# Scores in pairs of tiles, a split mean square, half rows of x from two queues, and later small products in a two-layer encoder

## The reference

```python
for i in range(DEPTH):                       # DEPTH = 2
    h = (_chunked_spatial_gating if i % 2 == 0 else _diff_attention)(x, ...)
    x = _layer_norm(DEEPNORM_ALPHA * x + h, ln_g[i, 0], ln_b[i, 0])
    h = _conv_glu_ffn(x, ...)
    x = _layer_norm(DEEPNORM_ALPHA * x + h, ln_g[i, 1], ln_b[i, 1])
# the attention, per head h (8 heads) with two halves j of 64 channels:
logits = einsum('bqhjd,bkhjd->bhjqk', q, k) + bias
probs = softmax(logits);  attn = probs[:, :, 0] - lam * probs[:, :, 1]
o = einsum('bhqk,bkhe->bqhe', attn, v)
o = o * rsqrt(mean(square(o), axis=-1) + LN_EPS) * subln_g * (1 - lambda_init)
```

## Time and profile before

| | us |
|---|---|
| median of 3 runs | 1295.48 (1295.4 to 1296.23) |
| profiled execution | 1295.56 |
| its span | 1293.9 |
| PE busy | 1277.3 |
| DVE busy | 637.0 |
| ACT busy | 456.7 |
| POOL busy | 158.6 |

### The profile page before, as it was taken

The page is one execution under the profiler, slowest core; times in us unless marked ns, Lnnn a source line. Parts: engine busy times, 40 slices in busy tenths (PEclk is TensorE's granted clock), DMA queues, the critical chain, the costliest instruction groups (busy, mean ns, idle before and its releaser), DMA issues.

```text
span 1293.9 us, 15596 instructions
## 1 busy us (share of the span) xinstructions
PE 1277.3 (99%) x6078; PEld 1051.6 (81%) x6078; DVE 637.0 (49%) x879; ACT 456.7 (35%) x545; POOL 158.6 (12%) x159
## 2 busy tenths in 40 slices
PE   8999999999999999999999999999999999999997
PEld 6788888889888888888888777788888888888886
DVE  3627877346343434433463566664743434343346
ACT  3422333322232323322314677776132323232230
POOL 3001100040000000000315442434200000000001
PEclk9999999999999999999999999999999999999999
DMA  8334563250322332222513334234132223323221
GB/s 300 105 98 115 176 174 139 93 184 1 130 97 97 97 97 97 98 97 94 166 58 92 105 88 114 82 115 152 44 98 97 97 97 96 99 93 102 94 101 65
DMA packets 103931, 140.62 MB, mean 109 GB/s; under 512 B 9360, under 2 KB 81128, under 8 KB 103632
## 3 DMA queue, kind: packets, MB, share of 16 engines
q1 hardware_dynamic: 94304, 127.67, 30.5%
q0 software_dynamic: 9440, 12.11, 2.9%
q10 hardware_dynamic: 144, 0.26, 0.1%
HBM read 137.85 MB, written 10.52 MB: 115 GB/s over the span
## 4 chain that ended last, share of the span: by engine, by line
PE 94%; DVE 4%; issue 1%; ACT 1%; DMA 0%; SPq 0%; DVEq 0%; ACTq 0%
PE bank L1208 31%; PE bank L1212 30%; PE bank L1211 30%; PE bank L1570 1%; PE bank L1224 1%; PE bank L1430 1%; DVE xt_lo L731 1%; PE bank L1594 1%; DVE x_tok L785 1%; DVE r_stat L754 0%; ACT xt_hi L436 0%; DMA w_raw<-in_a_w_in_dram 0%; DVE x_tok L748 0%; DVE x_tok L776 0%; PE bank L1433 0%
## 5 line engine op out<-in xcount | busy, mean ns | idle before, releaser
L1208 PE MATMUL bank<-xt_hi,w_hi 128*128 128x512 f32 (+1 forms) x1008 | 383.3, 380 | 0.4 <-DVE xt_lo L731 0.4
L1212 PE MATMUL bank<-xt_hi,w_lo 128*128 128x512 f32 (+1 forms) x1008 | 378.9, 376 | 0.0
L1211 PE MATMUL bank<-xt_lo,w_hi 128*128 128x512 f32 (+1 forms) x1008 | 378.8, 376 | 0.0
L726 DVE TENSOR_TENSOR w_lo<-w_raw,w_hi 128x2048 fp32r<-128x2048 f32 x79 | 180.8, 2288 | 190.5 <-ACT w_hi L431 164.1
L1208 PEld LDWEIGHTS bank<-xt_hi,w_hi 128*128 128x128 f32 x1008 | 189.7, 188 | 36.6 <-issue 3.0
L1211 PEld LDWEIGHTS bank<-xt_lo,w_hi 128*128 128x128 f32 x1008 | 189.8, 188 | 35.3 <-issue 1.4
L1212 PEld LDWEIGHTS bank<-xt_hi,w_lo 128*128 128x128 f32 x1008 | 189.7, 188 | 34.5
L431 ACT CAST w_hi<-w_raw 128x2048 fp32r<-128x2048 f32 x53 | 101.2, 1912 | 191.2 <-PE bank L1208 188.6
L1208 PE MATMUL bank<-w_hi,s_hi 128*128 128x512 f32 x416 | 162.5, 391 | 0.0
L1212 PE MATMUL bank<-w_hi,s_lo 128*128 128x512 f32 x416 | 161.9, 389 | 0.0
L1211 PE MATMUL bank<-w_lo,s_hi 128*128 128x512 f32 x416 | 161.9, 389 | 0.0
(11 more groups left out here) (191 smaller groups left out, 1411.9 us busy)
## 6 DMA issues: line engine op xcount, KB each, us to landing
w_raw<-in_f_w_in_dram SPq DMA_DIRECT2D x44, 1024.0 KB, 5.1
w_raw<-in_f_w_down_dram SPq DMA_DIRECT2D x22, 1024.0 KB, 4.8
w_raw<-in_a_w_in_dram SPq DMA_DIRECT2D x14, 1024.0 KB, 5.9
bias_by_query_key<-bias_by_distance POOLq DMA_DIRECT2D x8, 1024.0 KB, 15.5
w_raw<-in_a_w_out_dram SPq DMA_DIRECT2D x8, 1024.0 KB, 4.9
w_raw<-in_b_w_qkv_dram SPq DMA_DIRECT2D x16, 512.0 KB, 5.1
bias_sb<-bias_by_query_key SPq DMA_DIRECT2D x32, 256.0 KB, 2.6
w_raw<-in_b_w_qkv_dram SPq DMA_DIRECT2D x4, 1024.0 KB, 5.2
```

The source lines that it names most:

```text
L726: dve.tensor_tensor(lo_of(u), w_raw[:, u % 2, :], hi_of(u), ALU.subtract).then_inc(w_lo_done, 1)
L1208: ins = pe.matmul(o, a_hi, b_hi, start=start, stop=False)
L1211: pe.matmul(o, a_hi, b_lo, start=False, stop=False)
L1212: return pe.matmul(o, a_lo, b_hi, start=False, stop=stop)
```

## The change

- `scores` of two tiles stand next to each other in PE's list, in four banks (2 and 3 for even tiles, 1 and 4 for odd ones); each waits for the tile two before it. Query and key are projected into banks 0 and 2. DVE's and ACT's lists are reordered to match; on ACT `query_key(1, 0)` now stands ahead of `exps(0, 3)`.
- The squares are written twice by ACT, fp32 and as a high part in float32r; DVE makes the low part (`square_lo`), and the mean square is two float32r products with float32r `ones`, in bank 0 (in bank 4 for the last two heads). They lie in the buffers of `at_hi` and `at_lo`, so `probs_hi` waits for `ms_mm`.
- The value pairs of heads 4 and 5 use banks 5 and 6, those of heads 6 and 7 both bank 0.
- x comes in half rows (2 KB), the first halves of tiles 0 and 1 from ACT's queue, the others from SP's between the weight pieces. PE, ACT and DVE take halves: PE's first part works through growing squares of tiles and channel blocks (`highs`, `lows`).
- The bias table's product is split in high and low (two float32r products for one fp32 product), and `small_products` stands in the middle of token group 2, in banks 4 to 6.
- POOL's low half of a unit is sliced between the `shares` of a head.

```diff
+        def query_key_bank(c):
+            return bank[2 * c]
+        def score_bank(t, j):
+            return bank[(1, 4)[j] if t % 2 else 2 + j]
+        def pair_bank(n):
+            return bank[5 + n - TB if n < TB + 2 else 0]
+        def square_bank(h):
+            return bank[0 if h < H - 2 else 4]
+        def squares_of(h):
+            return (sq_hi, sq_lo) if h < H - 2 else (sz_hi, sz_lo)
...
-            sp.dma_start(x_tok[:, 0, :], xv[0]).then_inc(x_landed[0], 16)
-            for c in range(4):
-                sp.dma_start(raw(0, NB)[:, c:c + 1, :], cols(a_w_in[0], WIDTH, NB, c, 1)).then_inc(w_piece[c], 16)
-            sp.dma_start(x_tok[:, 1, :], xv[1]).then_inc(x_landed[1], 16)
-            for c in range(2):
+            def x_half(t, h):
+                sp.dma_start(x_tok[:, t, NB * h:NB * h + NB], xv[t, :, NB * h:NB * h + NB]
+                             ).then_inc(x_landed[TB * h + t], 16)
+            def second_unit(c):
                 sp.dma_start(raw(1, NB)[:, 2 * c:2 * c + 2, :], cols(a_w_in[0], WIDTH, NB, 4 + 2 * c, 2)
                              ).then_inc(w_piece[4 + c], 16)
-            for t in range(2, TB):
-                sp.dma_start(x_tok[:, t, :], xv[t]).then_inc(x_landed[t], 16)
+            for c in range(4):
+                if c >= 2:
+                    x_half(c, 0)
+                sp.dma_start(raw(0, NB)[:, c:c + 1, :], cols(a_w_in[0], WIDTH, NB, c, 1)).then_inc(w_piece[c], 16)
+            x_half(0, 1)
+            second_unit(0)
+            second_unit(1)
+            for t in range(1, TB):
+                x_half(t, 1)
             load_tokens_side(a_w_in[0], WIDTH, U_AV, N_AV, 2)
...
+            def x_half(t, h):
+                act_e.wait_ge(turned, TB * h + t + 1)
+                act_e.copy(xt_hi[:, 4 * h:4 * h + 4, t * P:t * P + P],
+                           bank[4 + t][:, :].rearrange("p (k n) -> p k n", n=P)).then_inc(xt_hi_done, 1)
+            for t in range(2):
+                act_e.dma_start(x_tok[:, t, 0:NB], x[0].rearrange("(t p) d -> t p d", p=P)[t, :, 0:NB]
+                                ).then_inc(x_landed[t], 16)
+            for t in range(TB):
+                piece(t)
+                x_half(t, 0)
+            x_half(0, 1)
             piece(4)
             piece(5)
-            for t in range(2, TB):
-                split_rows(0, t)
+            for t in range(1, TB):
+                x_half(t, 1)
...
-                act_e.activation(o_sq[:, :], bank[7][:, :], ACT.Square).then_inc(sq_done, 1)
+                act_e.activation(o_sq[:, :], bank[7][:, :], ACT.Square)
+                if h >= H - 2:
+                    act_e.wait_ge(mixp_done, TB * (H - 1) + 1)
+                act_e.activation(squares_of(h)[0][:, :], bank[7][:, :], ACT.Square).then_inc(sq_hi_done, 1)
...
             weights(U_QK1)
+            values_hi(TB)
             exps(0, 0)
-            values_hi(TB)
             exps(0, 1)
+            values_hi(TB + 1)
             exps(0, 2)
-            values_hi(TB + 1)
+            query_key(1, 0)
             exps(0, 3)
             weights(U_QK1 + 1)
-            query_key(1, 0)
...
                 exps(h + 1, 1)
-                query_key(h + 2, 0)
                 exps(h + 1, 2)
                 squares(h)
+                query_key(h + 2, 0)
                 exps(h + 1, 3)
                 root(h)
...
+            def square_lo(h):
+                dve.wait_ge(sq_hi_done, h + 1)
+                hi, lo = squares_of(h)
+                dve.tensor_tensor(lo[:, :], o_sq[:, :], hi[:, :], ALU.subtract).then_inc(sq_lo_done, 1)
...
+            def turn_half(t, h):
+                pe.wait_ge(x_landed[TB * h + t], 16)
+                if t == h == 0:
+                    pe.wait_ge(ident_done, 1)
+                if h:
+                    pe.wait_ge(xt_lo_done, t + 1)
+                for k in range(4 * h, 4 * h + 4):
+                    ins = pe.transpose(bank[4 + t][:, k % 4 * P:k % 4 * P + P], x_tok[:, t, k * P:k * P + P],
+                                       ident[:, :])
+                ins.then_inc(turned, 1)
+            def cells(n):
+                return [(n, k) for k in range(n + 1)] + [(t, n) for t in range(n)]
+            def cell(t, k, rows, cols, start=False):
+                pe.matmul(bank[t][:, :], rows[:, k, t * P:t * P + P], cols[:, 0, k * NB:k * NB + NB], start=start,
+                          stop=False)
+            def highs(n):
+                pe.wait_ge(xt_hi_done, n + 1)
+                if n < 3:
+                    pe.wait_ge(piece_hi, n + 1)
                 else:
+                    pe.wait_ge(w_hi_done, 1)
+                for t, k in cells(n):
+                    cell(t, k, xt_hi, w_hi, k == 0)
+            def lows(n):
+                if n < 3:
+                    pe.wait_ge(piece_lo, n + 1)
                 else:
+                    pe.wait_ge(w_lo_done, 1)
+                for t, k in cells(n):
+                    cell(t, k, xt_hi, w_lo)
+                pe.wait_ge(xt_lo_done, n + 1)
+                for t, k in cells(n):
+                    cell(t, k, xt_lo, w_hi)
+            for n in range(TB):
+                turn_half(n, 0)
+                if n:
+                    lows(n - 1)
+                highs(n)
+            turn_half(0, 1)
+            turn_half(1, 1)
+            lows(TB - 1)
...
+                    pe.matmul(bank[5 + c][0:H, :], tab_hi[:, :], hits, start=True, stop=False)
+                    ins = pe.matmul(bank[5 + c][0:H, :], tab_lo[:, :], hits, start=False, stop=True)
...
-                        pe.wait_ge(qk_lo_done, 2 * h - 1 + c)
+                    if h == 0:
+                        pe.wait_ge(bv_lo_done, 2 * c + 1)
+                    elif c == 1:
+                        pe.wait_ge(sc_done, 2 * TB * (h - 1) + 5)
+                    elif h < 3:
+                        pe.wait_ge(qk_lo_done, 2 * h - 1)
                     else:
-                        pe.wait_ge(bv_lo_done, c + 1)
-                ins = blocks(bank[c], u, c, 2 * P, 0, S, frees, ks)
...
-                    if n >= 2:
-                        pe.wait_ge(sc_done, n - 1)
+                    if n >= 4:
+                        pe.wait_ge(sc_done, n - 3)
...
             def mean_square(h):
-                pe.wait_ge(sq_done, h + 1)
-                if h >= 1:
+                pe.wait_ge(sq_lo_done, h + 1)
+                if h < H - 2:
+                    pe.wait_ge(qk_lo_done, 2 * h + 5)
+                else:
+                    pe.wait_ge(sc_done, 2 * TB * H)
+                if h == H - 1:
                     pe.wait_ge(ln_done, h)
-                pe.matmul(bank[4][:, :], ones[:, :], o_sq[:, :], start=True, stop=True).then_inc(ms_mm, 1)
+                hi, lo = squares_of(h)
+                pe.matmul(square_bank(h)[:, :], ones[:, :], hi[:, :], start=True, stop=False)
+                pe.matmul(square_bank(h)[:, :], ones[:, :], lo[:, :], start=False, stop=True).then_inc(ms_mm, 1)
...
-            for t in range(TB):
-                value_pair(U_V45, 4, t, 1 if t == 0 else 0)
+            for t in range(0, TB, 2):
+                value_pair(U_V45, t, 1 if t == 0 else 0)
+                value_pair(U_V45, t + 1)
                 scores(0, t)
+                scores(0, t + 1)
             project(1, 0, range(KD), 1)
             project(1, 1, range(KD))
             for h in range(H - 2):
                 turn_probs(h, 0, 1)
                 turn_probs(h, 1)
-                project(h + 2, 0, range(0, 2))
+                project(h + 2, 0, range(0, 3))
                 turn_probs(h, 2)
+                turn_probs(h, 3)
                 scores(h + 1, 0)
-                turn_probs(h, 3)
-                project(h + 2, 0, range(2, 5))
                 scores(h + 1, 1)
+                project(h + 2, 0, range(3, 6))
                 values(h, 0)
-                project(h + 2, 0, range(5, KD))
+                values(h, 1)
                 scores(h + 1, 2)
-                values(h, 1)
+                scores(h + 1, 3)
                 values(h, 2)
-                scores(h + 1, 3)
                 values(h, 3)
-                project(h + 2, 1, range(0, 3))
+                project(h + 2, 0, range(6, KD))
+                project(h + 2, 1, range(0, 4))
                 mean_square(h)
-                project(h + 2, 1, range(3, KD))
+                project(h + 2, 1, range(4, KD))
             h = H - 2
             turn_probs(h, 0, 1)
             turn_probs(h, 1)
-            value_pair(U_V67, 0, 0)
+            value_pair(U_V67, 0)
             turn_probs(h, 2)
+            turn_probs(h, 3)
             scores(h + 1, 0)
-            turn_probs(h, 3)
-            value_pair(U_V67, 0, 1)
             scores(h + 1, 1)
-            value_pair(U_V67, 0, 2)
+            value_pair(U_V67, 1)
             scores(h + 1, 2)
-            value_pair(U_V67, 0, 3)
             scores(h + 1, 3)
...
             for h in range(1, H):
-                weights(U_QK1 + h + 1)
```

(14 more changed lines are left out.)

275 lines of the change are left out of this document (121 added, 154 removed).

## The result

The changed kernel takes 1286.6 us (median) against 1295.5. That is 8.9 us less by the medians; the ratio is 0.9934, with a 95% interval of 0.9922 to 0.9946, more than the 0.2% of 2.6 us that counts as a change. One of the five executions took 2130.67 us at a mean granted clock of 0.557; it is a slow one and left out of the ratio. The prediction was 1284.9 us with 1281.5 to 1289.0: the median lies inside, 1.7 us above the forecast. The profiled execution took 1286.26 us, its span is 1284.6 us, 9.3 less than before; so the comparison of traces has 9.3 us to explain, not 8.9.

What follows compares the result with a forecast made beforehand. TensorE, busy 99% of the span, was taken as the bound. The terms 0.84 + 9.3 + 1.15 + 0.8 + 1.6 - 3.0 gave 10.7 us off 1295.56, so 1284.9 us, range 1281.5 to 1289.0.

Steps and rivals of the forecast that it cites:

- Middle heads: Six middle heads of attention: 1.55 us saved in each, from 20.94 to 19.4 us, 9.3 us in all.
- two joints: Middle heads: four groups of scores become two, saving 0.42 us per group's entry and exit, 0.84 us a head.
- mean square: Each head: two float32r products of 0.45 us replace an fp32 product of 0.87; gain 0.41 a head.
- third group's wait and the other joints: Middle heads: the wait for a score bank goes, 0.20 us; joints between transposes, values and the rest give about 0.1.
- rival 5: Mean square's new wait in all six middle heads makes the kernel slower; 1299.9 us at 2.5 us a head; chance 0.03.
- Head 0: Opening stretch: the weight cast moves behind head 1's query cast on ACT, so PE waits 3.0 us at `project(2, 0)`.
- pairs of head 0: Opening stretch: pairing head 0's score tiles saves 2 x 0.42 = 0.84 us.
- The clock: Head 0's wait: the forecast sum had no clock fall there, as 3.0 us is less than 3.9; rival 3 had it.
- rival 3: Clock falls in head 0's 3.0 us wait; half rate costs 1.6 to 4.3 us, 1286.5 to 1289.2; chance 0.12.
- Last stretch: Head 6's transposes to head 7's mean square: 1.7 us saved less waits of 0.25 and 0.3; gain 1.15.
- Start: Work up to 36.17 us: unbroken work and clock rise about 1 us earlier, two joints less; 1.6 us gained, an estimate.
- Small products: Four fp32 records of 0.43 us become four float32r products of 0.227; 0.8 us gained.

Runs made afterwards that it cites:

- e5_split: e1_order with the two score tiles of each pair taken apart again on PE in the six middle heads; 1287.8 us.
- e6_fp32: e1_order with the mean square and the bias table by distance as fp32 products again, the splits left in unused; 1287.0 us.
- e1_order: Changed kernel with head 0's last exponentials and weight cast QK1+1 again ahead of head 1's query cast on ACT, DVE splitting that query last; 1282.2 us.
- e7_spq: e1_order with the first halves of x tiles 0 and 1 issued by SP instead of ACT; 1282.1 us.
- e4_wait2: Order of e1_order plus two needless POOL operations between pieces of unit QK1+1's low half, to lengthen PE's wait; 1285.6 us.
- e2_fill: Changed kernel plus 11 needless products on PE ahead of the product that waits for unit QK1+1 in head 0; 1285.85 us.
- e8_warm: Order of e1_order plus 18 needless transposes of ident on PE before x lands; 1281.1 us.
- e9_warm14: As e8_warm with 14 needless transposes instead of 18; 1280.2 us, 0.9887 of the kernel before.

## Why the prediction was right, and where it was off

It was right in sign and place, and 1.4 us off in the profiled pair (10.7 foretold, 9.3 measured). The terms were worked out on a profile, so that is where they are compared.

- **Middle heads.** 19.4 us foretold, 19.48 measured: 1.49 instead of 1.55 a head, 8.9 in place of 9.3. e5_split prices the two joints at 0.88 (mine 0.84), e6_fp32 the mean square at 0.47 (mine 0.41). What is left for the third group's wait and the other joints is 0.1, where I had 0.3: this term was too large by 0.2 a head, and the other two make up for half of it. That the sum came so near is in part luck. The chain to the mean square had 0.5 us of slack by my count, and PE shows no wait there: rival 5 didn't come.
- **Head 0.** I worked out that the product would come 3.0 us late; it came 2.89 late (2.64 of it PE idle), on ACT and POOL where I put it. With the old order on ACT and DVE the wait is gone (e1_order), and PE's releaser was POOL, POOL's was ACT's cast. The pairs of head 0 brought 0.9 for 0.84.
- **The clock.** This term is most of the miss. The step that failed is the one in rival 3, "3.0 is less than 3.9": I took the single idle time of the end of the run at which the clock stood lower as the bound from which it falls, but that row says only that 3.9 us were enough there, not that less are not. It fell behind 2.64 us, and not in the profile with 1.99. Rival 3's price of at least 1.6 is what it cost, 1.61; so what happened is my forecast with rival 3's lower end, 1286.5 us against 1286.6 measured. I gave it 0.12. That the two times agree to 0.1 us is luck, since the other terms' errors cancel.
- **Last stretch.** 1.35 us for 1.15. Behind the second pair of scores PE is idle for 0.14 us, the wait for `values_lo`, and the product comes 0.21 late (mine 0.25); `values(7, 0)` waited for nothing (mine 0.3), while the split of head 6's output made PE idle for 0.24 us ahead of an `out_unit`, a product 0.49 late. With these delays the stretch should have gained 1.0; where the other 0.35 us come from the rows don't say.
- **Start.** 1.6 foretold, 1.8 in the profiled pair, about 0.9 on average, though the first half tile lands at 4.89 us, later than the whole tile before (4.27). I gave the gain to the work being unbroken sooner, and the rise of the clock with it. That the rise itself wanders, and moves the start by up to 1 us from run to run, wasn't in the sum; that the profiled pair came near 1.6 is luck.
- **Small products.** 0.8 for 0.8.

The miss in the profiled pair, 1.4 us, is thus 1.6 (clock) + 0.4 (heads) - 0.2 (start) - 0.2 (last stretch) - 0.1 (delay) - 0.1 (pairs of head 0). The medians are 8.9 us apart and not 9.3; a start that varies by up to 1 us is enough for that.

The Trainium skill (DMA: Bandwidth & Descriptors, "Issuing engines are not separate DMA queues"), which the prediction weighed, says that a second queue saves issue time alone. e7_spq agrees in the time, 1282.1 and 1282.2 us. But the landing differs by 1.3 us, against the queue of ACT: here the second queue brought the first half tile later.

What stays open: each length of the wait has one profile, and the other runs of e4_wait2 leave it open whether a wait of 2.0 us makes the clock fall in some of them. The moment of the fall varied too. The start's rise was seen to vary without a cause that the profile names.

## What to carry over

When an edit moves an instruction in a queue, count what stands behind it there: one query cast ahead of one weight cast cost this kernel 4.4 us (1286.6 against 1282.2), half as much as the whole change brought, while ACT was idle for 3.8 us just before. A wait of a full TensorE can have two prices: the wait itself and, behind the 2.64 and 3.20 us of this kernel but not in the profiles with 0.76 and 1.99, 1.6 us for the clock; useless products in the gap, or before the first data lands, buy back 1.5 us in the profile of e2_fill (0.8 by its median), and 1.1 to 2.1 us in e8_warm and e9_warm14. Where a timeline's first microseconds run at the lower level, take the gain there from several profiles.
